# Norm factor applied after two products, a second expert product of 384 columns, and gathered rows for the whole last prompt tile

## The reference

```python
x += W_out @ concat(diff_attention, retention)          # mixer
x += cross_attn(rmsnorm(x, g_cross), memory)            # 4 heads, 256 memory tokens
x += peer(rmsnorm(x, g_ffn))
y  = rmsnorm(x, g_final)

def rmsnorm(x, g): return x * rsqrt(mean(x * x) + EPS) * g

def peer(h):                                            # per token
    q = h @ w_pq                                        # 8 heads x 2 halves x 128
    s1, s2 = q1 @ keys1.T, q2 @ keys2.T                 # 128 keys each
    v1, i1 = top16(s1); v2, i2 = top16(s2)
    sc, pos = top16(v1[:, None] + v2[None, :])
    e = 128 * i1 + i2                                   # 16 experts of 16384, per head
    gate = softmax(sc)
    act = gelu(u_tab[e] . h)
    return sum(gate * act * v_tab[e])                   # 128 (head, slot) pairs per token
```

## Time and profile before

| | |
|---|---|
| three runs | 2149.8, 2143.61, 2148.0 us; median 2148.0 us |
| the profiled execution: its own time, its span | 2150.16 us, 2148.3 us |
| busy share of the span | PE 94%, PEld 91%, DVE 63%, ACT 36%, POOL 48% |
| mean granted TensorE clock | 0.974 |
| chain that ended last, by engine | PE 89%, DVE 4%, ACT 2%, SP's queue 1% |

### The profile page before, as it was taken

One profiled execution on the slowest core, in us unless ns is written; L12 is line 12 of the kernel. 1 busy time (PEld: TensorE's weight loads), 2 busy tenths in 40 slices (PEclk: granted clock), 3 DMA queues, 4 the chain that ended last, 5 costly groups with the idle time before them and its releaser, 6 DMA issues.

```text
span 2148.3 us, 38620 instructions
## 1 busy us (share of the span) xinstructions
PE 2018.7 (94%) x13914; PEld 1964.2 (91%) x13914; DVE 1356.3 (63%) x2421; ACT 783.2 (36%) x1281; POOL 1036.2 (48%) x821
## 2 busy tenths in 40 slices
PE   5999997788979999999999999988999999999998
PEld 4888887787868899999999999988999999999997
DVE  6444444633469779899999932212258788888864
ACT  5434433233233443444433433323333333333332
POOL 3222122323232578688778877500176676765300
PEclk9999998899989999999999999998999999999997
DMA  5644522022145344444444444424669999999971
GB/s 190 193 153 130 175 87 86 20 99 68 50 151 169 98 136 135 135 133 133 131 133 131 135 135 135 135 68 145 251 239 357 351 348 347 358 355 351 344 273 42
DMA packets 186332, 381.64 MB, mean 178 GB/s; under 512 B 34560, under 2 KB 104352, under 8 KB 186144
## 3 DMA queue, kind: packets, MB, share of 16 engines
q1 hardware_dynamic: 148896, 313.50, 42.6%
q0 software_dynamic: 37376, 67.46, 9.1%
HBM read 310.44 MB, written 70.21 MB: 177 GB/s over the span
## 4 chain that ended last, share of the span: by engine, by line
PE 89%; DVE 4%; ACT 2%; SPq 1%; issue 1%; POOL 1%; DMA 1%; DVEq 0%; ACTq 0%; POOLq 0%
PE bank L877 27%; PE bank L879 27%; PE bank L878 26%; PE bank L939 1%; PE bank L1240 1%; PE bank L1146 1%; DVE mixedT L1760 1%; PE bank L930 1%; PE bank L1174 1%; DVE rmo L1882 1%; PE bank L984 1%; DVE sq_sum L1731 1%; DVE rms L1750 0%; PE bank L953 0%; DMA wring<-in_v 0%
## 5 line engine op out<-in xcount | busy, mean ns | idle before, releaser
L877 PE MATMUL bank<-h_hi,u_hi 128*128 128x272 f32 x3136 | 919.9, 293 | 72.7 <-DVE h_lo L1754 27.6
L879 PE MATMUL bank<-h_hi,u_lo 128*128 128x272 f32 x3136 | 914.2, 292 | 0.0
L878 PE MATMUL bank<-h_lo,u_hi 128*128 128x272 f32 x3136 | 908.7, 290 | 0.0
L877 PEld LDWEIGHTS bank<-h_hi,u_hi 128*128 128x128 f32 x3136 | 597.8, 191 | 85.2 <-issue 34.9
L878 PEld LDWEIGHTS bank<-h_lo,u_hi 128*128 128x128 f32 x3136 | 598.4, 191 | 0.5
L879 PEld LDWEIGHTS bank<-h_hi,u_lo 128*128 128x128 f32 x3136 | 596.4, 190 | 0.0
L799 POOL DMA_INDIRECT scratch_gates<-total,gidx x416 | 476.8, 1146 | 126.1 <-issue 126.1
L1984 DVE TENSOR_TENSOR u_lo<-wring,u_hi 128x1024 fp32r<-128x1024 f32 x252 | 307.8, 1222 | 238.1 <-ACT u_hi L1620 235.1
L1620 ACT ACTIVATE u_hi<-wring 128x1024 fp32r<-128x1024 f32 x271 | 286.2, 1057 | 397.5 <-PE bank L879 352.1
L716 POOL TENSOR_TENSOR u_lo<-wring,u_hi 128x1024 fp32r<-128x1024 f32 x72 | 171.5, 2383 | 475.8 <-ACT u_hi L1354 400.1
L877 PE MATMUL bank<-w_hi,u_hi 128*128 128x416 f32 x1016 | 358.5, 353 | 0.0
(11 more groups left out here) (260 smaller groups left out, 1748.2 us busy)
## 6 DMA issues: line engine op xcount, KB each, us to landing
wring<-in_u SPq DMA_DIRECT2D x128, 512.0 KB
wring<-in_v SPq DMA_DIRECT2D x128, 512.0 KB
scratch_act<-actb SPq DMA_DIRECT2D x128, 272.0 KB, 2.1
scratch_gates<-zeros SPq DMA_DIRECT2D x64, 416.0 KB, 5.0
a<-scratch_act SPq DMA_DIRECT2D x32, 832.0 KB, 7.9
g<-scratch_gates SPq DMA_DIRECT2D x32, 832.0 KB, 10.4
wring<-in_w_in SPq DMA_DIRECT2D x28, 512.0 KB, 3.8
wring<-in_w_x SPq DMA_DIRECT2D x24, 512.0 KB, 5.6
```

Source lines behind the costliest of these rows:

```text
L877: pe.matmul(out, whi, xhi, start=first, stop=False)
L878: pe.matmul(out, whi, xlo, start=False, stop=False)
L879: return pe.matmul(out, wlo, xhi, start=False, stop=last)
```

## The change

1. Cross queries and PEER queries are made from x * gain, rounded and split as each block of the residual is done (`low_of_x`, `as_split`), without 1/rms. The sum of squares goes through PE behind the first query block. 1/rms is applied by DVE to the cross queries (`queries`: two tensor_tensor in place of two copies), and by ACT as a scale per token to the PEER scores (nine activations per head in place of three; `rcol` holds 1/rms with tokens on partitions). The normed h that the first expert product needs is formed on the side (`hx`) and put into `hs` chunk by chunk during the last query block.
2. ND goes from 416 to 384: the dense table and the second product cover the first three prompt tiles only. The whole fourth tile becomes sparse: NB goes from 4 to 5 batches, rows from 128 to 160, scatters from 416 to 384, and the packing of the quarter tile (`pack`) goes.
3. Rows begin at tile 10 instead of 14 and stand every 0.6875 tiles (110/160) instead of every 0.8125 (104/128); the ring has 6 buffers instead of 4. The first rows no longer wait for the end of the first product.
4. The spreading DMAs (48, now 60) move from SP's queue, where they stood after group 28 of the first product, to POOL's, after the last scatter.

The diff, cut to its core; first the sizes:

```diff
-ND = 416
+ND = 384
+NTD = ND // P
-BATCH_ROW = tuple(range(ROWS3, P, NG)) + (0,)
-NB = len(BATCH_ROW)
+BATCH_OF = tuple((0, row) for row in range(0, P, NG)) + ((1, 0),)
+NB = len(BATCH_OF)
-VROWS = 4
+VROWS = 6
-ROW_FROM = 14
-ROW_EVERY = (KEYS - 10 - ROW_FROM) / NROWS
-SHUFFLE = 28
+ROW_FROM = 10
+ROW_EVERY = (KEYS - 8 - ROW_FROM) / NROWS
```

On SP:

```diff
-            sp.wait_ge(h_ready, C * (NORM_FFN + 1))
-            sp.wait_ge(odd_ready, 3 * C // 2)
+            sp.wait_ge(xo_taken, 2 * C + 2)
...
-            with sp.Fori(0, SHUFFLE - U1_GROUPS) as i:
+            with sp.Fori(0, KEYS // GROUP - 1 - U1_GROUPS) as i:
                 first_group(i + U1_GROUPS, d["u"], i + (U1_GROUPS + 1), False)
-            sp.wait_ge(samp_ready, 1)
-            for k in range(KG):
-                to, src = slice(NG * k, NG * k + NG), slice(STEPS * k, STEPS * k + STEPS)
-                for b, row in enumerate(BATCH_ROW):
-                    rows = slice(row, row + NG)
-                    sp.dma_start(eidx[to, b], eu[rows, src]).then_inc(shuf_landed, 16)
-                    sp.dma_start(gk[to, b], gk_of[rows, src]).then_inc(shuf_landed, 16)
-                    sp.dma_start(aidx[to, b], au[rows, src]).then_inc(shuf_landed, 16)
-            with sp.Fori(0, KEYS // GROUP - 1 - SHUFFLE) as i:
-                first_group(i + SHUFFLE, d["u"], i + (SHUFFLE + 1), False)
```

On POOL:

```diff
             low_block(N_XQ, XQ, 0)
-            low_odd(1)
...
-            CELLS = [(p, t, k) for p in range(PH) for t in range(NT - 1) for k in range(SLOTS_OF[t])]
+            CELLS = [(p, t, k) for p in range(PH) for t in range(NTD) for k in range(TOPK)]
-                        pack(p)
...
+            pool.wait_ge(samp_ready, 1)
+            for k in range(KG):
+                to, src = slice(NG * k, NG * k + NG), slice(STEPS * k, STEPS * k + STEPS)
+                for b, (of, row) in enumerate(BATCH_OF):
+                    rows = slice(row, row + NG)
+                    pool.dma_start(eidx[to, b], eu[rows, of, src]).then_inc(shuf_landed, 16)
+                    pool.dma_start(gk[to, b], gk_of[rows, of, src]).then_inc(shuf_landed, 16)
+                    pool.dma_start(aidx[to, b], au[rows, of, src]).then_inc(shuf_landed, 16)
             pool.wait_ge(shuf_landed, 16 * KG * 3 * NB)
-            pool.wait_ge(unit_done, 4 + 2 * (NPQ + KEYS))
             for n in range(VROWS):
                 gather_row(n)
```

On PE:

```diff
+            def as_split(outs, slot, before, done, of, free=False):
+                for c in range(C):
+                    pe.wait_ge(xl_ready, before + c + 1)
+                    for h in range(2):
+                        m = product(outs[h][:, 0:HT], slot, c, h, c == 0, c == C - 1, of)
+                        if c == C - 1:
+                            m.then_inc(done, 1)
+                    if free and c < C - 1:
+                        m.then_inc(chunk_free, 1)
...
-            output_projection(N_WO, wo_taken, wo_done, MIXED_EARLY, MIXED_READY)
+            output_projection(N_WO, wo_taken, wo_done, MIXED_EARLY, MIXED_READY, hs)
+            halves_ready(N_XQ)
+            as_split(bank[2:4], 0, 0, x_done, h2)
             norm_sums(NORM_CROSS, T)
...
+                        n, outs = i * 4 + (2 * j + s), bank[2:4] if s == 0 else bank[0:2]
+                        halves_ready(n + FRONT)
+                        if first and j == 0 and s == 0:
+                            as_split(outs, 0, C, unit_done, hs)
+                            norm_sums(NORM_FFN, T)
+                            for t in range(NT):
+                                rows = TILES[t][1]
+                                m = pe.matmul(bank[7][0:rows, HT + t:HT + t + 1], sq_sum[:, tile_cols(t)],
+                                              ones[:, 0:1], start=True, stop=True)
+                            m.then_inc(sums_ready, 1)
+                        elif last and j == 1 and s == 1:
+                            pe.wait_ge(unit_taken, n * 2 + 2)
+                            as_split(outs, 1, C, unit_done, hs, free=True)
```

On ACT:

```diff
                     act.wait_ge(taken, 2 * m + 4)
+                    act.activation(to[0][:, m], xT[:, m], ACT.Copy, scale=gains[:, k, m:m + 1]).then_inc(xh_ready, 1)
                     squares(C * k + m, xT[:, m], T, m % 2)
-                roots(k, T)
...
-                    for s in range(2):
-                        act.activation(mine[:, s, 0:4].rearrange("p t n -> p (t n)"), bank[4 + s][:], ACT.Copy)
+                    for t in range(NT - 1):
+                        for s in range(2):
+                            act.activation(mine[:, s, t], bank[4 + s][:, t * P:(t + 1) * P], ACT.Copy,
+                                           scale=rcol[:, t:t + 1])
```

On DVE:

```diff
+            def low_of_x(k, highs, c, to):
+                dve.wait_ge(xh_ready, highs + c + 1)
+                dve.scalar_tensor_tensor(out=to[1][:, c], in0=xT[:, c], scalar=gains[:, k, c:c + 1],
+                                         in1=to[0][:, c].bitcast(F32), op0=ALU.mult,
+                                         op1=ALU.subtract).then_inc(xl_ready, 1)
...
-                dve.tensor_copy(xqT[:, 0], qrT[:])
-                dve.tensor_copy(xqT[:, 1], krT[:]).then_inc(xq_ready, 1)
+                dve.tensor_tensor(xqT[:, 0], qrT[:], rms[:], ALU.mult)
+                dve.tensor_tensor(xqT[:, 1], krT[:], rms[:], ALU.mult).then_inc(xq_ready, 1)
...
+            for c in range(C):
+                dve.scalar_tensor_tensor(out=hx[c], in0=xT[:, c], scalar=gains[:, NORM_FFN, c:c + 1], in1=rms[:],
+                                         op0=ALU.mult, op1=ALU.mult).then_inc(hx_ready, 1)
...
+                if p == 1:
+                    for c in range(C):
+                        dve.wait_ge(xh_ready, 2 * C + c + 1)
+                        dve.tensor_tensor(hs[1][:, c], hx[c], hs[0][:, c].bitcast(F32), ALU.subtract).then_inc(xl_ready, 1)
```

More of the change, by code:

```diff
@@ L178, in encoder_step @@
         lam = plan.place("lam", [P, 4])
+        rcol = plan.place("rcol", [P, NT])
         wring = plan.place("wring", [P, SLOTS, C, P])
@@ L297, in encoder_step @@
         assert spare.end <= plan.end
+        over_w = Plan(nc, plan.start_of["wring"] + 4 * 4 * C * P)
+        hx_w = over_w.place("hx_w", [P, 5, T])
+        assert over_w.end <= plan.end
+        hx = [hx_w[:, c] for c in range(5)] + [sq[:, 0], sq[:, 1], sq_sum[:]]
         ret = Plan(nc, late_at)
@@ L1548, in _, with query_unit @@
             blocks = [((b + 1) % 4, 16 * (2 * HEADS + 1 + b // 4)) for b in range(2, C)]
-            output_highs(NORM_CROSS, wo_taken, wo_done, blocks + [(XQ + b, 16 * (HEADS + 1)) for b in range(2)])
-            high_halves(1)
-            act.activation(table, eps[:, 0:1], ACT.Exp)
+            output_highs(NORM_CROSS, wo_taken, wo_done, blocks + [(XQ + b, 16 * (HEADS + 1)) for b in range(2)], h2)
             xq_next = (qrT, krT)
-            def query_unit(turn, k):
+            def query_unit(turn, k, first=False):
                 b, h = k // 2, k % 2
                 act.wait_ge(x_done, turn * 4 + (k + 1))
-                act.activation(xq_next[b][:, half(h)], bank[h][:, 0:HT], ACT.Copy).then_inc(x_taken, 1)
+                out = bank[h] if b or not first else bank[2 + h]
+                act.activation(xq_next[b][:, half(h)], out[:, 0:HT], ACT.Copy).then_inc(x_taken, 1)
             def block_after(turn, b):
@@ L1601, in _ @@
             for k in range(4):
-                query_unit(0, k)
+                query_unit(0, k, True)
                 if k % 2:
                     block_after(0, k // 2)
+                if k == 1:
+                    roots(NORM_CROSS, T)
+                    act.activation(table, eps[:, 0:1], ACT.Exp)
             with act.Fori(0, HEADS - 1) as i:
@@ L1635, in two_heads @@
                         high(i * 8 + (2 * b + 4), (b + 1) % 4, i * 16 + 16 * (PQ_TURN[(b + 1) % 4] + (b == 3)), us[0][(b + 1) % 2])
+                        if last and b == 3:
+                            act.wait_ge(hx_ready, C)
+                            for c in range(C - 1):
+                                act.wait_ge(chunk_free, c + 1)
+                                act.activation(hs[0][:, c], hx[c], ACT.Copy).then_inc(xh_ready, 1)
                         for h in range(2):
                             act.wait_ge(unit_done, i * 8 + (4 + 2 * b + h + 1))
-                            act.activation(qpT[:, s, half(h)], bank[(2 * b + h) % 4][:, 0:HT],
+                            act.activation(qpT[:, s, half(h)], bank[(2 * b + h + 2) % 4][:, 0:HT],
@@ L1639, in two_heads @@
                                            ACT.Copy).then_inc(unit_taken, 1)
+                        if first and b == 0:
+                            roots(NORM_FFN, T)
+                            for rows, t in ((slice(0, P), slice(0, NT - 1)), (slice(0, TS), slice(NT - 1, NT))):
+                                a = act.activation(rcol[rows, t], bank[7][rows, HT + t.start:HT + t.stop], ACT.Sqrt,
```

(2 more changed lines are left out.)

230 lines of the change are left out of this document (119 added, 111 removed).

## The result

The changed kernel takes 2112.8 us (median of 4 runs, 2112.0 to 2115.2) against 2148.9 (4 runs): a ratio of 0.9837, with an interval of 0.9825 to 0.9849. It is faster, by 36 us where 22 were forecast (2127), inside the range of 2075 to 2163. The profiled execution took 2115.2 us, with a span of 2113.4, 34.9 less than before.

A forecast was written before the change was run, and what follows sets the result against it. PE was taken to bound both expert products, with POOL taking over the second after the change; 2150.2 - 15 - 13 - 22 + 27 + 2.4 = 2129.6 us profiled, so 2127 us, range 2075 to 2163.

The forecast's parts named there:

- Cross norm: Mixer projection's end to first cross scores: gain 17.0 us, less 2 in the later heads, net -15.
- PEER norm: Wait before the first PEER scores: gain 15 us, less 2 for more score copies on ACT, net -13.
- DVE's lateness: PEER norm: `lo` halves behind two heads of top-16 could make PE wait up to 5.8 us; counted as nothing.
- Spreading: First expert product: small DMAs no longer hold SP's table load, and cost nothing on POOL; -22 us.
- Columns: Second product: 32 fewer columns per matmul make PE's tile 4.18 instead of 4.52 us, 43 us over 128 tiles.
- Second product: All 128 tiles: 58 to first batch + 403 rows + 20 batches + 125 behind = 606 against 579, +27 us.
- The pair: POOL in the second product: one row and one activation issue take 3.15 us, 403 us for 128 rows.
- the waits at the batches: Second product: DVE waits for each later batch's last activation behind POOL's pairs; 4 x 5 = 20 us.
- Fold: A fourth batch to fold costs a third of 7.11 us, +2.4.
- The DMA engines: Rival, second product: 1680 kB a tile at 372 GB/s take 4.52 us; +3, 2103 us in all; chance 0.18.
- The lock-out: Rival, tiles 10 to 98: DVE locks POOL out, 3.5 us a pair, 651 us stage, 2172 in all; chance 0.17.
- PE as the bound: Rival, second product: POOL needs only 2.5 us a pair, PE sets the pace; -34, 2066 us; chance 0.13.

The follow-up runs named there:

- the first three edits: Both norm edits and the spreading on the kernel before, with 416 columns and four batches kept: 2103.6 us, ratio 0.9795.
- fewer bytes: Changed kernel, loads of activations and gates for the second product bring one tile of every four from the third group on: 2106.9 us, one run.
- the even list: Changed kernel with gate multiplies in pieces of 8, 16 activations first, then activation and row by turns, rows from tile 5 every 0.75 tiles: 2067.0 us, ratio 0.9622.
- each half alone: Changed kernel with gate multiplies in pieces of 8, plus only rows from tile 5 every 0.75 tiles (2091.3 us) or only POOL's alternating list (2098.1 us).
- the fourth: The change's columns and rows, with the ring and the rows' start: 2112.8 us with it, 2103.6 us for the changed kernel's other edits without it.

## Why the prediction was right, and where its sizes were off

The mechanism was right: the first three edits pay, and POOL takes the second product over from PE. The forecast of 2127 us is 14 too high, and nearly all of this is one term, the second product. By steps, from the profiles of before and after:

- Cross norm, -15 forecast. From the mixer's last reciprocal to the first cross score 84.9 us became 67.3: 17.6 gained (17.0 forecast). The heads from first to last score took 90.2 and take 92.8: 2.6 lost (2 forecast). Net -15.0.
- PEER norm, -13. From the last cross score to the first PEER score 96.2 became 80.0: 16.2 gained (15). From the first PEER score to the last, 113.6 became 115.7: 2.1 lost (2). The step that counted nothing for the handover to the first product was 2.5 too low: PE waits 2.6 instead of 1.6 us for ACT there, and its granted clock is 0.98 instead of 1.00 in the 80 us behind it. Net -11.6. So DVE's lateness, kept for the range, didn't come, and the copies on ACT cost a little more.
- Spreading, -22: 21.8 in the kernel that has this edit alone.
- Columns: DVE's `w_lo` comes every 4.16 us where PE sets the pace (1504.11, 1508.27), 4.18 forecast.
- Second product, +27 for all 128 tiles. Measured +13: 580.7 before (562.6 and four tiles of 4.52), 594.0 after (577.3 and four of 4.18). By parts: 50.4 to the first batch (58 forecast), 418.2 for 128 rows (403 + 20), 125.5 behind the last batch (125). The term that was mis-sized is the start. The forecast kept the 58 us of before, in which POOL issued four rows and waited 3.6 us ahead of the first activation. Now the ring doesn't share its place with the first product's operands any more, so the first rows are issued at 1349.88, long before, and the activations start 5.8 us behind PE's start instead of 10.4. The text of the change showed the wait that goes; the sum didn't use it. Besides, the last of the 32 activations take 0.95 us each beside a DVE that already waits, so that all of them take 44 us, not 50. The rest of the difference is 5 us at the batches, and 2 us by which the start of before was put too late.
- The pair: 3.15 forecast, 418.2/128 = 3.27 with the waits at the batches, 1.28 + 1.33 + 2 x 0.30 = 3.21 without. So the pair was taken about 8 us too cheap over 128 rows, and the waits at the batches, 20 us in the sum and some 7 in the trace, 13 too dear. That 403 + 20 came within 5 us of 418.2 is partly luck.
- Fold: 3.2 (2.4 forecast).
- Not in the forecast: the mixer ran 3.1 us faster in the profiled execution after. It differs as much between runs of the same code, so this part of the gain is chance.

The sum: -15.0 - 11.6 - 21.8 + 13.3 + 3.2 - 3.1 = -35.0, against -34.9 of the spans.

The rivals. The DMA engines: by the time alone this rival can't be told apart, since 2112.8 us lies at the upper end of its range (2085 to 2112). But fewer bytes changed little, and 398 GB/s were reached, so 372 was what was asked for and no ceiling. The lock-out: DVE does stretch POOL's issues (0.95 us where it stands, 1.10 with less of its work, 1.30 with all). The Trainium skill (SBUF — State Buffer, "Who interferes with whom") has this for DVE instructions with two SBUF inputs beside a GpSimd instruction that reads SBUF. Its inference that a tensor_tensor doesn't hold up descriptor generation doesn't fit these indirect issues: the kernel that shortened one tensor_tensor brought the issue from 1.30 to 1.10 us. But the mean didn't rise as DVE's gaps closed (1.31 and 1.30), which the price of 3.5 us a pair supposed; the argument against it, that a late row opens gaps in DVE, held. PE as the bound: not with this list, though the even list comes within 13 us of it (531.5 against 124 x 4.18 = 518).

What the prediction did not see is that its bound was one of order and place. It took 403 us for 128 pairs as POOL's rate. But 314 issues at 1.6 us are 502 us, less than PE's 535; POOL had to start early, never stand, and have its last row near the end.

## What to carry to other kernels

When an engine off the path comes close to the bound, take its total of work over the whole stage against the path's, not only its rate at one place: if the total fits, the loss is idle time, also that behind its last piece of work, and the list and the places of its consumers can be moved until it is hardly ever idle. Two lists that wait for each other must be moved together: each half alone took 7 us off the second product, both 32. A change of several edits is worth timing in parts: three of these gave 44 us, and the fourth took 9 back.

## What the runs showed of the hardware

The share of the DMA engines says little on their ceiling: it stood at 0.99 with 372 GB/s, and at 1.03 with 398 GB/s without the later activations. After PE's stall of 8.8 us in the changed kernel, which ends at 1648.75, PE runs at a granted clock of 0.50 (1.2 of 2.4 GHz) for at least 3 us, ten matmuls where nineteen stand a little later (windows, columns as in the earlier trace rows):

```profile
1649.00:1652.00 3.00, 3.00 (x10) 3.00 (x11) 3.00 (x5) 1.48 (x2) 2.35 (x2) 0.50 0.89 328
1654.00:1657.00 3.00, 3.00 (x19) 3.00 (x18) 2.90 (x4) 1.25 (x2) 2.69 (x2) 1.00 0.85 277
```

These 3 us lose about 1.5 us. The first 3 us behind each of the other four long waits (6.3 to 11.2 us) have the same clock of 0.50. In the even kernel, whose stalls are 2.1 us at most, the granted clock stays at 1.00 from 1600 to 1900 us. The length of a stall alone doesn't decide it: in the changed kernel one of 1.8 us, which ends at 1621.44, is followed by a stretch at 0.55.

```profile
1622.00:1625.00 3.00, 3.00 (x12) 3.00 (x11) 3.00 (x5) 1.58 (x2) 2.65 (x2) 0.55 1.03 391
```
